# Earlier weight splits at the start, one earlier fetch behind the gates, and attention tiles taken head by head

## What is computed

```python
def rms_norm(x, w):                       # first_block, its first step
    xf = x.astype(jnp.float32)
    y = xf * lax.rsqrt(jnp.mean(xf * xf, axis=-1, keepdims=True) + EPS)
    return (y * w.astype(jnp.float32)).astype(x.dtype)
...
h = rms_norm(x, mix_norm_w[l])
proj = jnp.einsum('bsd,de->bse', h, w_in[l])
...
# peer_ffn: every token has 8*16 experts; here up-products for all 16384 experts
act = jax.nn.gelu(jnp.einsum('td,ted->te', hb, u), approximate=False)
return jnp.einsum('te,ted->td', gb * act, v)
...
# dsa_mixer (second_block), per block of 128 queries and 8 heads
logits = (jnp.einsum('bqhc,bqkc->bqhk', qb_lat, kv_sel) + bias)
logits = jnp.where((dist >= 0)[:, :, None, :], logits, -jnp.inf)
p = jax.nn.softmax(logits, axis=-1)
return jnp.einsum('bqhk,bqkc->bqhc', p, kv_sel)
...
o = jnp.einsum('bthc,hcv->bthv', o_lat, w_uv)
return o @ w_o
```

## Time and profile before

| | us |
|---|---|
| time, median of 3 runs | 2905.5 (2904.29 to 2907.15) |
| the profiled execution's own time | 2909.46 |
| its span, first to last instruction | 2907.7 |
| PE busy | 2759.3 (95%) |
| DVE busy | 1890.3 (65%) |
| ACT busy | 1195.7 (41%) |
| POOL busy | 536.7 (18%) |
| mean granted TensorE clock | 0.983 |

### The profile page before, as it was taken

One profiled execution on the slowest core, in us unless ns is written; L12 is line 12 of the kernel. 1 busy time (PEld: TensorE's weight loads), 2 busy tenths in 40 slices (PEclk: granted clock), 3 DMA queues, 4 the chain that ended last, 5 costly groups with the idle time before them and its releaser, 6 DMA issues.

```text
span 2907.7 us, 36988 instructions
## 1 busy us (share of the span) xinstructions
PE 2759.3 (95%) x14045; PEld 2343.5 (81%) x14045; DVE 1890.3 (65%) x3534; ACT 1195.7 (41%) x1928; POOL 536.7 (18%) x393
## 2 busy tenths in 40 slices
PE   8999999989998999999998999999999978999997
PEld 6777878878777999998997888888887546788876
DVE  3334665765565778877975888888885674544434
ACT  5545243233223454447993333333333444422322
POOL 0112220220000787771000111111110021000000
PEclk9999999999999999999999999999999989999999
DMA  4112101003562587765768989998883101222220
GB/s 160 51 51 86 60 30 44 30 30 131 217 217 114 201 300 280 271 236 191 284 231 308 336 319 346 337 350 324 334 304 131 30 30 44 80 97 92 87 102 29
DMA packets 141359, 501.19 MB, mean 172 GB/s; under 512 B 13400, under 2 KB 67072, under 8 KB 111616
## 3 DMA queue, kind: packets, MB, share of 16 engines
q1 hardware_dynamic: 122752, 364.60, 35.0%
q0 software_dynamic: 18432, 134.23, 11.8%
HBM read 450.53 MB, written 48.25 MB: 172 GB/s over the span
## 4 chain that ended last, share of the span: by engine, by line
PE 80%; DVE 9%; ACT 5%; DMA 3%; issue 2%; POOL 1%; SPq 0%; DVEq 0%; ACTq 0%; POOLq 0%
PE bank L244 21%; PE bank L246 21%; PE bank L245 21%; PE bank L2154 2%; DVE xn L1532 1%; PE bank L2743 1%; PE bank L1107 1%; PE bank L740 1%; PE bank L1117 1%; PE bank L1123 1%; DMA w_raw<-in_w_in_dram 1%; DVE M L2946 1%; DVE m L2942 1%; PE bank L346 1%; DVE whl L240 1%
## 5 line engine op out<-in xcount | busy, mean ns | idle before, releaser
L244 PE MATMUL bank<-HH,uhl 128*128 128x384 f32 x1024 | 349.9, 342 | 9.0 <-DVE uhl L1658 7.1
L246 PE MATMUL bank<-HH,uhl 128*128 128x384 f32 x1024 | 346.7, 339 | 0.0
L245 PE MATMUL bank<-HL,uhl 128*128 128x384 f32 x1024 | 346.6, 339 | 0.0
L244 PE MATMUL bank<-vhl,awhl 128*128 128x512 f32 x768 | 300.0, 391 | 6.7 <-DVE awhl L2372 4.7
L246 PE MATMUL bank<-vhl,awhl 128*128 128x512 f32 x768 | 299.8, 390 | 0.0
L245 PE MATMUL bank<-vhl,awhl 128*128 128x512 f32 x768 | 299.5, 390 | 0.0
L1714 POOL DMA_INDIRECT gs<-in_uv_dram,idx x128 | 151.6, 1185 | 776.0 <-DVE x L1739 481.6
L2312 ACT ACTIVATE vhl<-vraw 128x1024 fp32r<-128x1024 f32 x128 | 135.7, 1061 | 317.3 <-PE bank L246 281.8
L1658 POOL TENSOR_TENSOR uhl<-ur,uhl 128x1024 fp32r<-128x1024 f32 x69 | 167.7, 2439 | 321.1 <-ACT uhl L1652 320.8
L244 PE MATMUL bank<-HH,whl 128*128 128x512 f32 x528 | 215.8, 409 | 5.9 <-DVE whl L240 4.1
L240 DVE TENSOR_TENSOR whl<-w_raw,whl 128x2048 fp32r<-128x2048 f32 x49 | 113.5, 2317 | 160.2 <-ACT whl L234 160.1
(11 more groups left out here) (421 smaller groups left out, 6197.3 us busy)
## 6 DMA issues: line engine op xcount, KB each, us to landing
ur<-in_peer_u_dram SPq DMA_DIRECT2D x128, 512.0 KB, 5.5
vraw<-in_peer_v_dram SPq DMA_DIRECT2D x128, 512.0 KB, 5.9
w_raw<-in_w_in_dram SPq DMA_DIRECT2D x36, 1024.0 KB, 5.0
xn<-in_ada_rows_dram SPq DMA_DIRECT2D x48, 512.0 KB, 4.5
g_scratch<-stg SPq DMA_DIRECT2D x12, 2048.0 KB, 8.1
gti<-g_scratch SPq DMA_DIRECT2D x16, 1536.0 KB, 11.5
wf_raw<-in_f_w_in_dram SPq DMA_DIRECT2D x22, 1024.0 KB, 4.8
act_scratch<-ag SPq DMA_DIRECT2D x96, 192.0 KB, 2.7
```

What stands on the lines that cost most here:

```text
L244: e.matmul(out, l[0], r[0], start=start, stop=False)
L245: e.matmul(out, l[0], r[1], start=False, stop=False)
L246: return e.matmul(out, l[1], r[0], start=False, stop=stop)
```

## The change

Three independent parts.

1. First norm: ACT loads the table set that holds the square root as its first instruction. Weight 0 is split ahead of all 8 column tiles on ACT and on DVE, where it stood between the third and fourth tile.
2. Behind the gates: `sp_u(95)` stands right behind `sp_save(90)`; it stood after a wait for all gates, a wait for the saved gates, and the transfers of `act 0`, `gti 0`, `v 0`, `v 1` and `act 1`.
3. Second mixer: tile g is head g // 4 and block 0, 3, 1, 2 in turn. `pe_ol(h, 0)` stands at step 4h + 7, `pe_ol(h, 1)` at 4h + 8, `pe_ov(h)` at 4h + 10; ACT's copies at 4h + 8, 4h + 9 and 4h + 11; `dve_ov(h)` at 4h + 12. The waits name the head's last tile 4h + 3.

```diff
+SQRT_SET = "sqrt_and_others"
...
     def act_norm1(e):
         T, A, V, G = N1
+        e.preload_act_table_set(SQRT_SET)
...
-        high_x(e, T, A, R1, lambda kt: vcol("mix_norm_w", kt), range(3))
         split_hi(e, W, 0)
-        high_x(e, T, A, R1, lambda kt: vcol("mix_norm_w", kt), range(3, KT))
+        high_x(e, T, A, R1, lambda kt: vcol("mix_norm_w", kt), range(KT))
...
-        low_x(e, A, V, R1, lambda kt: vcol("mix_norm_w", kt), range(3))
         split_lo(e, W, 0)
-        low_x(e, A, V, R1, lambda kt: vcol("mix_norm_w", kt), range(3, KT))
+        low_x(e, A, V, R1, lambda kt: vcol("mix_norm_w", kt), range(KT))
...
     def sp_gates(e):
...
-        sp_save(e, up_end[0])
+        sp_up(e, up_end[0])
         all_done(e, *GT)
         sp_act(e, 0)
...
         sp_act(e, 1)
-        sp_u(e, up_end[0] + 5)
         sp_v(e, 2)
...
     def item(g):
-        return 2 * (g // 8) + g % 2, g % 8 // 2
+        return g // 4, (0, 3, 1, 2)[g % 4]
...
     def act_ql(e, h):
-                e.wait_ge(*T.of("sc", 8 * ((h - 4) // 2) + 6 + h % 2))
+                e.wait_ge(*T.of("sc", 4 * (h - 4) + 3))
...
     def pe_ol(e, h, ct):
-        e.wait_ge(*A.of("pt", 8 * (h // 2) + 6 + h % 2))
+        e.wait_ge(*A.of("pt", 4 * h + 3))
...
     def pe_dsa(e):
-            if s >= 10:
-                p, i = divmod(s - 10, 8)
-                if i < 4:
-                    pe_ol(e, 2 * p + i // 2, i % 2)
-                if i in (3, 5):
-                    pe_ov(e, 2 * p + (i == 5))
+            if s % 4 == 3 and 7 <= s < 39:
+                pe_ol(e, (s - 7) // 4, 0)
+            if s % 4 == 0 and s >= 8:
+                pe_ol(e, (s - 8) // 4, 1)
+            if s % 4 == 2 and s >= 10:
+                pe_ov(e, (s - 10) // 4)
...
     def act_dsa(e):
-            if s >= 11:
-                p, i = divmod(s - 11, 8)
-                if i < 4:
-                    act_ol(e, 2 * p + i // 2, i % 2)
-                if i in (3, 5):
-                    act_ov(e, 2 * p + (i == 5))
+            if s % 4 == 0 and s >= 8:
+                act_ol(e, (s - 8) // 4, 0)
+            if s % 4 == 1 and s >= 9:
+                act_ol(e, (s - 9) // 4, 1)
+            if s % 4 == 3 and s >= 11:
+                act_ov(e, (s - 11) // 4)
...
-        act_ov(e, 7)
         split_hi(e, W3, W_O + 2)
...
     def dve_dsa(e):
-            if s >= 11:
-                p, i = divmod(s - 11, 8)
-                if i in (3, 5):
-                    dve_ov(e, 2 * p + (i == 5))
+            if s % 4 == 0 and s >= 12:
+                dve_ov(e, (s - 12) // 4)
```

## The result

The changed kernel takes 2884.16 us (median of 4 runs, 2882.30 to 2884.55), the kernel before 2906.32 us beside it (4 runs, 2904.29 to 2911.39): 22.2 us less by the medians. The ratio, taken over the runs, is 0.9914 with a 95% interval of 0.9902 to 0.9926, which is 25 us. The forecast was 2880.0 us with a range of 2873 to 2892. The profiled execution took 2882.30 us, with a span of 2880.6 and a mean granted clock of 0.986; its forecast was 2884 us with a span of 2882.

A forecast was written before the change was run, and what follows sets the result against it. PE carries 80% of the chain, so only its idle time in three stretches could be won: 2.5 + 5.0 + 18.0 = 25.5 us, taken off the median of 2905.5, gives 2880.0 us, range 2873 to 2892.

The forecast's parts named there:

- The step on the clock: Start of the experts: PE's first 4.8 us run at half clock behind its idle time and lose 2.4 us.
- The cover: Experts: the lost 2.4 us are covered, as PE stood 3.3 us before v row 3 and this wait moves by 4.5.
- the prediction's own sign of being wrong: Behind the gates: the prediction would be wrong if the DMA waits of the experts stage stayed where they were.
- (a): Second mixer's loop, the fill: PE reaches step 8 at 2367.2 us, at half clock at the start.
- (b): Second mixer, steps 8 to 19: PE bounds at 11.65 us per head plus 0.15 per `pe_ov`, until 2402.6 us.
- (c): Second mixer, steps 20 to 34, without scores: DVE bounds at 8.3 us per head; PE ends `pe_ov(6)` at 2435.0 us.
- (d): Second mixer's end, last head's `pe_ol`, `pe_ov` and copies: 8.7 us, so PE starts with `w_o` at 2443.7 us.
- the rival of half clock: Rival, chance 0.11: half clock in the loop's thin part; second mixer gives only 9 to 11 us; 2888 to 2891 us.
- DVE's wait for ACT's part of the split: Sign for the second mixer's loop: DVE's wait at L2773 would be under 8 us.
- the fetch that isn't last: Rival behind the gates, chance 0.07: ACT waits as long for other transfers, part 2 gives 0 to 1 us; 2884 to 2885.
- half the gain: Rival, chance 0.04: other waits hide part 1 and the stall moves to the banks; parts 1 and 3 give half; 2890 us.
- the turns of PE and DVE: Rival, second mixer, chance 0.03: PE and DVE take turns, each head serialises, loop 147 us instead of 111.7; 2933 us.

The follow-up runs named there:

- after: The profiled execution of the changed kernel with all three parts: 2882.30 us (median of 4 runs 2884.16 us).
- e4_after: The changed kernel run again with nothing edited: 2885.66 us, ratio 0.9922 to the kernel before.
- e1_norm: The first part (first norm) alone on the kernel before: 2906.24 us, ratio 0.9997.
- e3_tiles: The third part (second mixer's tiles by head) alone on the kernel before: 2893.18 us, ratio 0.9952.
- e2_fetch: The second part (earlier fetch of block 95) alone on the kernel before: 2904.30 us, ratio 0.9986.
- before: The profiled execution of the kernel before the change: 2909.5 us.
- e9_no_bias: The changed kernel without the near keys' relative bias: POOL makes no bias tiles, DVE adds the mask alone; 2880.80 us, ratio 0.9906.
- e7_ov_same_step: The changed kernel with `dve_ov(h)` at step 4h + 11, the step of ACT's part, instead of one step later: 2887.74 us, ratio 0.9927.
- e6_splits: The kernel before with only the order of the splits of weight 0 changed: 2908.66 us (one execution).
- e5_load: The kernel before with only the table load put first: 2908.69 us (one execution).
- e8_rising: The changed kernel with a head's four blocks in the order 0, 1, 2, 3 instead of 0, 3, 1, 2: 2883.42 us, ratio 0.9912.

## Why the prediction was right, point by point

**First norm, forecast 2.5 us.** Right in kind: one load at the start, none near 7 us, and PE's transposes last. PE begins at 17.61 (after), 16.75 (e4_after) and 17.44 us (e1_norm) against the 17.2 forecast; 2.1, 3.0 and 2.3 us. Mis-sized were two terms. In after both came out late: the roots ended at 10.6 as against 10.05 us, for the squares waited for landings, and the 29 transposes took 5.67 and not 5.29 us. They end at 17.85 and not 17.1 us, and the start is off by only 0.4 us because the projection starts 0.24 us ahead of their modelled end. In e1_norm and e4_after the roots ended as forecast (10.0 and 10.1 us), and transposes of 6.13 and 4.66 us put the start at 17.44 and 16.75: near 17.2 by luck of the two. The claim that the gain is kept behind the stage stands by the first key product (944.5 to 942.1 us in e1_norm, with 944.0 in e3_tiles and 945.2 in e2_fetch, which lack the part). By times alone it is not shown.

**Behind the gates, forecast 5.0 us.** The gap to the experts shrank by 4.8 us in after, 5.7 in e4_after and 5.1 in e2_fetch, at the upper end of the 3.6 to 5 us forecast for the first matmul or just above it. Each wait came as named: none for weights at L1652, the store of block 91 ahead of the gelu of block 94, at 1544.25 us. The gates end 5.3 us sooner in that execution than in before's (3.2 unplanned, 2.1 of the first part); counted from their end it is 1549.6 us, in the range of 1549.4 to 1550.9. The step on the clock was half right. Half level came: PE's first ten expert matmuls take until 1552.98 us, 4.3 us where 2.3 is the full level's, so 2.0 us are lost, 2.4 forecast. The cover was smaller than said. PE's two stands ahead of the next v rows, in before and then in after:

```profile
1578.62 0.47 PE L244 MATMUL bank<-vhl,awhl 128*128 128x512 f32 x1 [3.16 <-DVE awhl L2372]
1586.15 0.47 PE L244 MATMUL bank<-vhl,awhl 128*128 128x512 f32 x1 [1.58 <-DVE awhl L2372]
```

```profile
1567.63 0.47 PE L245 MATMUL bank<-vhl,awhl 128*128 128x512 f32 x1 [0.25 <-DVE awhl L2371]
1575.16 0.47 PE L245 MATMUL bank<-vhl,awhl 128*128 128x512 f32 x1 [3.17 <-DVE awhl L2371]
```

The stand for v row 3 went, as forecast (3.16 to 0.25 us); the next one, for which the forecast had no term, grew from 1.58 to 3.17 us, and ACT still waits 6.75 us for the landing of v row 3, where it waited 6.43. Counted from the last gate matmul that landing comes 5.7 us sooner, but ACT comes to it sooner too. This is close to the prediction's own sign of being wrong, the DMA waits of the experts stage staying where they were. Of the gain, 1.2 us (e2_fetch) and 0.9 us (e4_after) were given back; in after the experts stage was 0.9 us shorter. There before's clock was at half once more, granted 0.50 from 1580 to 1583 us, behind the stand of 3.16 us, while after's was granted 1.00 from 1570 to 1582 us. The rule of the Trainium skill that idle time brings half clock (TensorE: Matmul & The Clock Gate, Part 1) is seen here in the 0.61 and 0.71 behind 5.8 us of idle time; by it alone the part was to give 2.6 us, and e2_fetch gave 4.1 by the times, with an interval (1.5 to 6.7 us) that holds both, and 3.9 by its landmarks, which speak for the cover.

**Second mixer, forecast 18.0 us (93.7 us for the loop).** Measured 94.9, 95.1 and 95.4 us. By steps, counted from the loop's start:

| | forecast | after |
|---|---|---|
| (a) step 8 begins | 17.2 | 17.8 |
| (b) step 19 ends | 52.6 | 54.4 |
| (c) `pe_ov(6)` ends | 85.0 | 86.2 |
| (d) from there to `w_o` | 8.7 | 8.7 |

Step (b) was mis-sized: a head takes 12.19 and not 11.80 us. The term is the wait of `pe_ov` for ACT's copy, 0.15 us in the forecast. In the timeline above the 256-key scores start at 2374.47 and `pe_ov` at 2375.85 us, 1.38 us apart where those scores need 0.86: the wait costs 0.52 us. The bracket says 0.35, because a group is shown longer than it keeps the next one back: the 512-key scores stand until 2374.52 us, and the transpose behind them starts at 2374.36. A wait's price is read from start to start. The fill (a) was 0.6 us longer than walked, at the same pace of DVE and half clock until 2350 us (granted 0.86 in the next 6 us). Step (c) came out 0.6 us shorter than walked, and its mechanism is half right: from 2394 to 2418 us DVE hardly stands, but `pe_ov` starts are 8.04 and 7.92 us apart against 8.3, and e9_no_bias, with short divisions, has 7.91 and 7.92. So PE's own 7.3 us and its wait of some 0.5 us for ACT's copy bound this part about as much as DVE does. PE's longest stand there is 1.1 us, the granted clock stays at 1.00, and the rival of half clock falls for this kernel; e7_ov_same_step shows how near it is. One sign was wrong: DVE's wait for ACT's part of the split was to be under 8 us and is 18.4. It was no measure of the loss. Timeline of DVE at the largest of them:

```profile
2426.28 0.69 DVE L2772 TENSOR_TENSOR HL<-bank,HH 128x512 fp32r<-128x512 f32 x1 [6.69 <-ACT HH L2767]
```

At 2419.2 us DVE has divided its last tile. It waits 6.7 us because it has nothing to do, and PE's 40 `pe_ol` matmuls run beside it. Idle time of an engine that isn't the bound costs nothing, and a sign has to be put on the engine that is.

**The sum.** Forecast were 25.5 us; the medians give 22.2, and the ratios 0.9922 and 0.9914 of about 2906 us give 22.7 and 25 us. The interval of the second, 21.5 to 28.5 us, holds the forecast's gain of 25.5. Besides the 1.2 us of the loop, one step of the forecast was unsound: it took the gains from one execution and subtracted them from a median 4 us below it, and the old loop isn't the same in each. It took 111.7 us there, and 111.9, 111.7, 109.9 and 108.7 us in e1_norm, e6_splits, e5_load and e2_fetch, which have the same loop. The cause is the clock. Here is each stretch from some 20 us behind the loop's start to the first `w_o` matmul, in before and in e2_fetch (columns as above):

```profile
2370.00:2461.70 91.70, 74.15 (x448) 58.41 (x446) 45.69 (x107) 42.07 (x103) 13.22 (x17) 0.93 0.01 1
```

```profile
2367.30:2456.00 88.70, 71.18 (x448) 55.18 (x446) 45.67 (x107) 42.25 (x103) 13.25 (x17) 0.96 0.01 2
```

PE's busy time alone differs by 3.0 us over the same 448 matmuls, as the loop does. The granted clock of this stretch is 0.93 in the three executions of 111.7 to 111.9 us, 0.94 in the one of 109.9 and 0.96 in the one of 108.7, and 1.00 with the new order, whose loop took 94.9 to 95.4 us each time. So the third part gives 13 to 17 us, by the execution, and 14 by the ratio.

**The rivals.** The half clock in the thin part, the fetch that isn't last, half the gain and the turns of PE and DVE all fell for the changed kernel. The last of them shows in e7_ov_same_step with 4.6 us and would have needed 3.2 us a head.

## What to carry to other kernels

Where no engine is full, put the consumer of a result one step behind its producer on each queue, and finish one group before the next is begun, and not two side by side: here that gave 15% of the loop, of which about a third came from the clock, which the stands no longer brought to half. The order of blocks inside a group counts too, by what stands between a result and its reader (e8_rising). A store or a fetch behind which a chain hangs goes ahead of bulk transfers on its queue, and behind nothing that waits; look for the next such entry at once, since the removed wait of 9.15 us was worth 2.4 us until the v row behind it had moved too. And take a gain from an execution off that execution's own time, not off a median of quicker ones.

## What the runs showed of the hardware

Three things I had not expected. A store of 192 KB, which lands 2.8 us after its issue in the median of the page, took 9.1 us (1535.12 to 1544.25) with gti, v rows and activations issued ahead of it. It is in the chain of the changed kernel:

```profile
1535.12 9.11 DMA act_scratch<-ag
```

The same 29 transposes at the start took 4.63, 5.29, 5.31, 5.67 and 6.13 us in five executions. The starts of the single ones say why: they follow each other at 0.21 us first and at 0.11 us from one of them on, and that change, by the factor between 1.2 and 2.4 GHz, came at 15.3, 16.6, 15.7, 16.9 and 17.2 us; the profile's record of the granted clock begins at just these times (the column of stretches shows 1.00 ahead of its first record, which the spacing contradicts). And the kernel before spreads over 2901.7 to 2911.8 us in 21 runs, the changed one over 2882.3 to 2886.5 in 9: the old loop's stands bring half clock at points and for times that differ, as the part on the sum shows and e1_norm, whose slowest `pe_ol` matmul took 439 ns against a median of 275, while the slowest of the new loop took 275:

```profile
L2743 PE MATMUL bank<-PT,crow x320: 272/275/439, 2363.6 to 2450.2; 128*128 128x128 f32 x160
```

```profile
L2742 PE MATMUL bank<-PT,crow x320: 272/275/275, 2355.0 to 2429.8; 128*128 128x128 f32 x160
```

That this is the whole of the spread is not shown; the up to 4 us between the first projection and the last gate vary in both kernels.
